# Long convolution and its spectra by four residues of time, conditioning sums on TensorE

## What is computed

```python
def long_conv(z, kf, bias):
    L = z.shape[1]
    zf = jnp.fft.rfft(z, n=2 * L, axis=1)
    y = jnp.fft.irfft(zf * kf[None], n=2 * L, axis=1)[:, :L]
    return y + z * bias

z = v
for o, gate in enumerate((x1, x2)):
    z = gate * long_conv(z, K[:, o], bias[o])
```

## Time and profile before

| | us |
|---|---|
| three runs | 3769.68, 3773.18, 3778.75 |
| median | 3773.18 |
| profiled execution, first to last instruction | 3769.4 |

### The profile page before, as it was taken

How to read it: one execution, slowest core, us unless ns; L and a number is a source line. 1 busy time by engine, 2 the same in 40 slices (tenths; PEclk the granted TensorE clock), 3 DMA queues, 4 the chain that set the end, 5 groups by cost and what they waited for, 6 DMA issues and landing times. The chain is left out here.

```text
span 3769.4 us, 52561 instructions
## 1 busy us (share of the span) xinstructions
PE 3569.6 (95%) x18752; PEld 3149.5 (84%) x18752; DVE 2572.5 (68%) x5870; ACT 1292.2 (34%) x2645; POOL 1294.1 (34%) x807
## 2 busy tenths in 40 slices
PE   6889899998989799999999999999899999999997
PEld 4679788887767688999999999999788888888886
DVE  6653044435644555899997878888488787777876
ACT  1110132221142311322237888888322222222222
POOL 1133122213222112477762222222145455444521
PEclk9899999999999899999999999999999999999998
DMA  6741222317652222588866999999988888888873
GB/s 261 299 135 41 91 76 87 114 61 254 220 192 93 76 67 70 212 280 267 277 217 220 279 273 287 277 283 281 269 306 301 304 301 303 302 311 309 307 261 117
DMA packets 495542, 818.07 MB, mean 217 GB/s; under 512 B 289063, under 2 KB 304200, under 8 KB 489577
## 3 DMA queue, kind: packets, MB, share of 16 engines
q1 hardware_dynamic: 112584, 364.53, 27.7%
q0 software_dynamic: 84368, 319.85, 24.2%
q10 hardware_dynamic: 298384, 131.09, 14.5%
HBM read 673.77 MB, written 141.59 MB: 216 GB/s over the span
## 5 line engine op out<-in xcount | busy, mean ns | idle before, releaser
L2381 POOL DMA_INDIRECT va_rows<-in_vtab,k_pick x256 | 460.7, 1800 | 546.6 <-DVE k_big L2548 421.9
L79 PE MATMUL va_fps<-va_vt_h,va_c_h 128*128 128x512 f32 x1536 | 602.2, 392 | 22.8 <-DVE va_vt_l L2526 13.1
L80 PE MATMUL va_fps<-va_vt_l,va_c_h 128*128 128x512 f32 x1536 | 601.2, 391 | 0.0
L81 PE MATMUL va_fps<-va_vt_h,va_c_l 128*128 128x512 f32 x1536 | 600.8, 391 | 0.0
L2548 DVE SCALAR_TENSOR_TENSOR k_big<-va_rows,va_coef,k_big 128x1024 f32<-128x1024 f32 x254 | 317.5, 1281 | 69.1 <-DMA va_rows<-in_vtab,k_pick 69.0
L79 PEld LDWEIGHTS va_fps<-va_vt_h,va_c_h 128*128 128x128 f32 x1536 | 290.7, 189 | 85.2 <-issue 8.6
L2198 ACT ACTIVATE ga_first<-ga_first,ga_gs 128x128 f16<-128x128 f16 x1152 | 356.5, 394 | 0.0
L80 PEld LDWEIGHTS va_fps<-va_vt_l,va_c_h 128*128 128x128 f32 x1536 | 290.7, 189 | 60.7
L81 PEld LDWEIGHTS va_fps<-va_vt_h,va_c_l 128*128 128x128 f32 x1536 | 290.5, 189 | 60.7
L2474 ACT ACTIVATE va_vt_h<-k_edge 128x1024 fp32r<-128x1024 f32 x128 | 135.8, 1061 | 560.3 <-PE va_fps L81 351.9
L2259 DVE TENSOR_SCALAR ga_second<-ga_iota,k_sel 128x128 f16<-128x128 f16 x768 | 198.3, 262 | 107.0 <-PE ga_ps L2160 103.9
(11 more groups left out here) (358 smaller groups left out, 8775.8 us busy)
## 6 DMA issues: line engine op xcount, KB each, us to landing
k_ut<-in_utab SPq DMA_DIRECT2D x128, 512.0 KB, 4.2
k_edge<-in_vtab SPq DMA_DIRECT2D x128, 512.0 KB
scratch_ahead<-k_gelu_a ACTq DMA_DIRECT2D x128, 384.0 KB, 2.6
k_edge<-scratch_ahead SPq DMA_DIRECT2D x128, 384.0 KB
k_edge<-scratch_gates SPq DMA_DIRECT2D x128, 384.0 KB
hy_tab<-in_tab POOLq DMA_DIRECT2D x64, 512.0 KB, 5.4
k_wada<-in_w_ada SPq DMA_DIRECT2D x24, 1024.0 KB, 7.6
scratch_gates<-k_edge ACTq DMA_DIRECT2D x32, 768.0 KB
```

The source lines that it names most:

```text
L79: nc.tensor.matmul(out, w[0], x[0], start=first, stop=False)
L80: nc.tensor.matmul(out, w[0], x[1], start=False, stop=False)
L81: return nc.tensor.matmul(out, w[1], x[0], start=False, stop=last)
L2381: nc.gpsimd.indirect_dma_start(got[:, q % SLOTS_G, :], None, vrows, picked(K, q)).then_inc(got_in[q % SLOTS_G], 16)
```

## The change

Time is sorted into four residues modulo 4 in place of two parities, and frequencies into orbits of four. A matmul then covers a quarter of the frequencies, and butterflies on VectorE make the four. In detail:

- `stage_spectra`: 288 matmuls in place of 384 for the transforms. They form four units (order and half), each of ten segments of 6 or 12 `product3` matmuls, taken two by two in five pairs, with a ring of six PSUM banks. The taps are made two tiles at a time, the matmuls of one on weight rows 0 to 63 and of the other on rows 64 to 127, in turn. The tables are loaded once (eight pieces of 0.5 MB in `stage_setup`) and kept. The bias of the long convolution is added to tap zero.
- Conditioning: the 24 steps leave VectorE. Each is 16 matmuls on TensorE with a 128 x 128 piece of `k_wada` as weights and one column of `silu(c)` as data, in plain float32. They stand behind the taps and behind the pairs (`BESIDE_TAPS`, `BESIDE_PAIRS`). The gates are spread along a row by `broadcast`, eight matmuls in two halves, each followed by an addition on VectorE.
- `stage_hyena`: two forward units per order of 48 matmuls, one VectorE unit for each with twice the frequencies, two subtractions of it on GpSimd (`BY_POOL`, L1126 and L1129 of the new file), an inverse of order 0 that leaves its result already turned (96 matmuls) and one of order 1 of 192 matmuls with 256 columns. The gate of order 0 is turned too (32 transposes). No bias term is left in `gate`.

```diff
+RESIDUES = (0, 2, 1, 3)
+RS = len(RESIDUES)
 def stage_spectra(nc, S, K, T):
+        UNITS, STEPS, RING = 4, 3 * KT, 6
+        PAIRS = 5
+        SEGMENTS = ((COS, (0,), 0), (COS, (1,), 0), (SIN, (0,), 1), (SIN, (1,), 1), (COS, (2, 3), 0), (SIN, (2, 3), 1),
+                    (SIN, (2,), 0), (SIN, (3,), 0), (COS, (2,), 1), (COS, (3,), 1))
+        BESIDE_TAPS = ((0, 0, 1, 1), (1, 1, 1, 1))
+        BESIDE_PAIRS = ((1, 1, 1, 1, 1), (1, 1, 1, 1, 1), (1, 1, 1, 1, 1), (1, 1, 1, 0, 0))
...
+            def ada(count):
+                for _ in range(count):
+                    e = next(steps)
+                    third, k = divmod(e, KT)
+                    pe.wait_ge(ada_in[e % ADA_BUFS], 16 * (e // ADA_BUFS + 1))
...
+                    for c in range(2 * KT):
+                        last = nc.tensor.matmul(ps[:, b, at + c:at + c + 1], wada[:, e % ADA_BUFS, c * P:(c + 1) * P],
+                                                K["silu"][:, k:k + 1], start=False,
+                                                stop=k == KT - 1 and c == 2 * KT - 1)
+                    last.then_inc(ada_used, 1)
...
+                    for n, (a, b) in enumerate((("h", "h"), ("h", "l"), ("l", "h"))):
+                        for st in range(2):
+                            last = nc.tensor.matmul(bank(st), h_of(st, a), f_of(st, b), start=n == 0, stop=n == 2)
...
+                for i in range(RS):
+                    taps(o, i)
+                    ada(BESIDE_TAPS[o][i])
+                if o == 1:
+                    broadcast(0)
+                pe.wait_ge(pm_ok, KT * (o + 1))
+                for j in range(2):
+                    for pair in range(PAIRS):
+                        for n in range(2 * pair, 2 * pair + 2):
+                            segment(o, j, n)
+                        ada(BESIDE_PAIRS[2 * o + j][pair])
+            broadcast(1)
...
-            def ada_step(e):
-                third, k = divmod(e, KT)
-                part = ada[:, third % 2, :]
-                dve.wait_ge(ada_in[e % ADA_BUFS], 16 * (e // ADA_BUFS + 1))
...
 def stage_hyena(nc, S, K, T):
...
+                pool.wait_ge(mult_ok, n + 1)
+                nc.gpsimd.tensor_tensor(work[:, 0, 0:RS, :], work[:, 0, 0:RS, :], work[:, 0, RS:2 * RS, :],
+                                        ALU.subtract).then_inc(p_ok, 1)
+                pool.wait_ge(p_ok, n + 1)
+                nc.gpsimd.tensor_tensor(work[:, 0, 6:8, :], work[:, 0, 0:4:2, :], work[:, 0, 1:4:2, :],
+                                        ALU.subtract).then_inc(apart_ok, 1)
+                for i in BY_POOL:
+                    pool.wait_ge(y_hi, RS * n + i + 1)
+                    nc.gpsimd.tensor_tensor(y_l[:, j, i, :, :], plain(i), y_h[:, j, i, :, :].bitcast(F32),
+                                            ALU.subtract).then_inc(y_lo_pool, 1)
...
+            forward(0, 0)
+            forward(0, 1)
...
+            inverse_turned(0)
+            inverse_turned(1)
+            forward(1, 0)
+            forward(1, 1)
+            pe.wait_ge(used, 8)
+            inverse(0)
+            inverse(1)
```

More of the change, by code:

```diff
@@ L287, in _ @@
[L287 to L343, removed]
@@ L445, in _ @@
-            take(2)
+                    tap_tile(o, lt)
+                    if lt % 2 == 1:
+                        tap_low(o, lt)
+                if o == 1:
+                    dve.wait_ge(ada_used, 2 * KT)
+                    columns(2 * KT, 3 * KT, 3 * KT)
+                    gain_columns(0, 2 * KT)
+                    gain_rows(0)
+                for j in range(2):
+                    unit(2 * o + j)
+                if o == 0:
+                    dve.wait_ge(ada_used, KT)
+                    columns(0, 2 * KT, 0)
@@ new lines, in forward @@
+            def forward(o, j):
+                for i in range(RS):
+                    g = o * PIECES + j * RS + i
+                    await_tab(g)
+                    if j == 1:
+                        pe.wait_ge(used, 4 * o + i // 2 + 1)
+                    for a in range(2):
+                        for st in range(2):
+                            if j == 0 and a == 0:
+                                pe.wait_ge(z_lo, o * KT + 2 * i + st + 1)
+                            cut = slice((2 * st + a) * P, (2 * st + a + 1) * P)
+                            last = product3(nc, ps[:, 2 * i + a, :], (tab[:, g % TS, 0, cut], tab[:, g % TS, 1, cut]),
+                                            (z_h[:, 2 * i + st, :], z_l[:, 2 * i + st, :]), st == 0, st == 1)
+                    last.then_inc(piece_mm, 1)
@@ L1142, in inverse @@
+            def inverse(j):
+                for pair in range(2):
+                    for i in (2 * pair, 2 * pair + 1):
+                        await_tab(PIECES + 2 * RS + j * RS + i)
+                        await_y(1, j, i)
                     for c in range(4):
                         cc = slice(c * P, (c + 1) * P)
[L1144 to L1146 removed]
@@ new lines, in inverse @@
+                        if j == 1:
+                            last.then_inc(inv, 1)
+                        elif c == 3:
+                            last.then_inc(piece_mm, 2)
+            for c in range(4):
+                pe.wait_ge(v_in[c], 16)
+            for k in range(KT):
+                turn(yh, k).then_inc(tp, 1)
+            forward(0, 0)
+            forward(0, 1)
+            for c in range(4):
+                pe.wait_ge(x_in[c], 16)
+            for k in range(KT):
+                if k % 4 == 0:
+                    pe.wait_ge(used, 2 + k // 4 + 1)
+                turn([xg[:, c, :] for c in range(4)], k).then_inc(x_tp, 1)
@@ new lines, in _ @@
+            z_low(KT - 1)
+            dve.wait_ge(z_lo, 2 * KT)
+            unit(2)
+            unit(3)
+            for pair in range(2):
+                for c in range(4):
+                    dve.wait_ge(inv, KT + 4 * pair + c + 1)
+                    dve.wait_ge(x_in[c], 32)
+                    v.tensor_tensor(by_residue(yh[c])[:, pair:RS:2, :],
+                                    ps[:, 2 * c + pair, :].rearrange("p (r s) -> p r s", r=2),
+                                    by_residue(xg[:, c, :])[:, pair:RS:2, :], ALU.mult)
```

636 lines of the change are left out of this document (329 added, 307 removed).

## The result

The changed kernel takes 3877.58 us (median of four runs, 3871.38 to 3882.73), the kernel before 3774.53 on the same chip: a ratio of 1.0272, interval 1.0260 to 1.0284. The forecast was 3866 us, slower, with a range of 3800 to 3905. The profiled execution spans 3869.6 us, 100.2 more than that of before; it belongs to the fastest of the four runs, and its span is 8.0 us under their median.

What follows compares the result with a forecast made beforehand. TensorE was taken to bound the kernel now, VectorE the changed Hyena stage. Spectra +83.5 and Hyena +9 on 3769.4 gave 3861.9 us profiled; with the median 3.8 above, 3866 us, range 3800 to 3905.

Steps and rivals of the forecast that it cites:

- units 0 and 1, ten steps: Spectra, order 0: eight pairs of 4.3, two of 7.05 and ten conditioning steps of 4.0 take 88.5 us.
- units 2 and 3, last broadcast, meeting: Spectra, order 1: pairs with eight steps, 80.5 us; then last butterflies, columns, broadcast and meeting of engines, 10.2.
- The price of a step and the clock: Conditioning on TensorE: a step costs 4.0 us, 6.8 at low clock, and the pair behind it starts low.
- full-clock rival: Spectra: TensorE's clock stays full through conditioning steps, so the stage loses only 25 us, 3807 in all; chance 0.13.
- 8 x 0.427 + 4 x 0.227 = 4.3: Spectra: 12 matmuls behind a conditioning step, eight at low clock, four at full, take 4.3 us.
- 4 x (2.6 + 6.8): Spectra, order 1 taps: four pairs of tiles at 2.6 us, each with a low-clock step of 6.8.
- The first term: Start of the spectra: 41.9 plus two tap pairs with low-clock steps, 18.8, so transforms begin at 60.7 us.
- Up to the third pair of tiles as now: Start of the spectra: work before the third pair of tap tiles keeps its timing, to 41.9 us.
- The nearly free step: Spectra: weights load beside the previous matmul, so conditioning steps hide between pairs; kernel faster, 3742 us; chance 0.08.
- 4.6 + 2 x 2.38: Hyena stage: GpSimd's subtraction and low parts add in full to each VectorE unit, 9.4 us.
- 32.5: Hyena stage: VectorE's own instructions in one new unit, in us, before GpSimd's share and links are added.
- The 24 steps that leave VectorE give nothing back: Spectra: taking conditioning off VectorE, some 56 us that nobody waits for, saves 0 us.

Runs made afterwards that it cites:

- half steps: Changed kernel with every second matmul of each conditioning step left out, 16 records a step in place of 32: 3789.02 us.
- tables first: Changed kernel with the Hyena stage's 2 MB spectrum and gate rows fetched only after the fourth table piece has landed: 3872.65 us.
- GpSimd's share moved: Changed kernel with all of GpSimd's subtractions of the Hyena stage given to VectorE: 3858.88 us.

## Why the prediction was right

It was right in sign and in mechanism, and 11.6 us (0.3%) low: 7.7 on the profiled execution, and the rest because the median lies 8.0 above it and not 3.8. That it came so near owes something to luck, since terms of the sum were off both ways. By the steps of its sum, forecast and profiled execution, in us:

| step | forecast | measured |
|---|---|---|
| transforms begin | 60.7 | 65.4 |
| units 0 and 1, ten steps | 88.5 | 93.6 |
| taps of order 1, broadcast | 43.6 | 34.5 |
| units 2 and 3, last broadcast, meeting | 90.7 | 92.8 |
| `stage_spectra` ends | 283.5 | 286.3 |
| `stage_hyena`, length | 217.8 | 216.0 |
| rest of the kernel | 0 | +6.7 |
| profiled execution | 3861.9 | 3869.6 |

- **The price of a step and the clock.** 4.07 us in the units and 6.96 to 6.98 beside the taps of order 0, where 4.0 and 6.8 were forecast. Leaving the steps out took both away; steps of 512 columns and half steps showed the clock's part by itself. The full-clock rival wants pairs of 2.7 us behind whole steps; one of them was that short (2.83 us, from 201.44), and no other of 12 was below 4.3.
- **Two terms were off, and cancelled.** "8 x 0.427 + 4 x 0.227 = 4.3" is about the best a pair of 12 did in the units of order 0, not its mean: they took 4.35 to 5.3, and so these units took 5 us more. "4 x (2.6 + 6.8)" for the taps of order 1 took 4 x 6.8 in the profiled execution: its steps there ran 3.9 to 4.0 us. In two other executions they ran 6.98 (last section), which is the forecast.
- **The first term was short.** The first taps begin at 33.7 and not 30.2. "Up to the third pair of tiles as now" took no account of a later start: 3.5 of the 4.7 us. In every run with the eight table pieces in `stage_setup` the taps begin between 32.9 and 33.9; what holds them up was not tried.
- **The nearly free step.** One column costs 0.112 us at full clock and 0.214 at the low one. The rule of the Trainium skill ("TensorEngine Tiling (Array Packing)", Instruction Overhead), one column as long as 60, gives 0.8 us a step as an estimate. The runs show 3.6 at best, so it does not price a stream in which each matmul loads 128 columns of weights.
- **The Hyena stage.** The exclusion of GpSimd and VectorE was the right reason for a stage that does not get faster with half of TensorE's work. Errors of both signs cancelled here. "4.6 + 2 x 2.38" left out GpSimd's second subtraction and counted the rest in full; VectorE's stretch is 8.6 us. The second unit took 40.3 us (1005.9 to 1046.2), not 42.6: 0.8 of that is the stretch, and most of the rest is that the durations of VectorE's rows reach into the next row (1.22 us long, 1.14 apart), so that 32.5 was too much. The four units are some 9 us shorter than forecast, the stage's head and the ends of the two orders some 7 longer. Not foreseen was the 3.5 us wait for the first table, behind a spectrum that is now fetched in one piece of 2 MB. Moving that fetch took the wait away.
- **"The 24 steps that leave VectorE give nothing back"** held for the changed kernel, where TensorE works without a gap and VectorE has 17 us of work in 94. It holds only while the matmuls are the bound: with 288 matmuls the same steps on VectorE cost about 30 us.
- **6.7 us in untouched stages** are not explained. Seven profiled executions with the same code in those stages took 3360.6 to 3367.3 us in them, the kernel before at the low end and the changed kernel the most.

## What to carry to other kernels

Price work that moves to another engine by what it does to that engine's clock as well as by its own time: a step of one-column matmuls, 3.6 us at full clock, took 4.3 in the mean and cost the stage 4.6, and of the 86 us that the stage lost 50 were the clock. If such products must go on TensorE, make the large operand the data, or keep each burst short; here the former still left the kernel 1.2% slower than before. Work that is hidden on a second engine is free only while the first stays the bound: once TensorE's matmuls were cut, the same steps on VectorE, with their sums, cost some 30 us (204.0 against 174.8), and two engines that exclude each other in instructions with two SBUF sources count as one while they do.

## What was not expected

The same code of the spectra ended at 286.3, 297.9 and 300.5 us in three profiled executions (the changed kernel, tables first, and GpSimd's share moved), though the units of order 0 took the same 94 us in each. Most of the difference is in one stretch, the taps of order 1 with their steps. In the last-named kernel, by stretch:

```profile
159.00:204.00 45.00, 43.16 (x193) 38.75 (x194) 22.22 (x19) 8.46 (x8) 9.42 (x4) 0.50 0.46 163
```

The same kernel's timeline of TensorE has one of the steps there, and the changed kernel's the one that answers to it:

```profile
162.24 6.98 PE L298 MATMUL sp_ps<-k_silu,k_wada 128*128 128x1 f32 x32
```

```profile
161.79 3.94 PE L298 MATMUL sp_ps<-k_silu,k_wada 128*128 128x1 f32 x32
```

In the changed kernel's profile the clock is low in each pair of taps and high in each step behind it; in the other two it is low in both, for 45 us. The order of the work is the same; about 10 us hang on where in it the clock comes back. This may be why the runs of the changed kernel spread over 11 us, and it is why small differences were read here from stages and not from totals. What decides between the two was not tried.
